# Two layer blocks on one core: the products that spread the HGRN norm's roots placed among a branch slot's products, and sixteen unread transposes ahead of the third norm's

## The reference, cut to what matters

```python
def hybrid_mixer(xn, ...):
    q, zf_fwd, zf_bwd, inp, og, hy, gates = split(xn @ w_in)
    o2 = hgrn2_chunk_scan(...)                  # forward and reversed
    o = o2[:B] + rev(o2[B:])
    o = rmsnorm(o, hgrn_norm_g).reshape(B, L, HGRN_WIDTH)    # over the 128 channels of each of 8 heads
    y_a = (o * silu(og)) @ w_branch_a
    y_b = (x0 * bidirectional_fftconv(v * x1, ...)) @ w_branch_b
    merged = sigmoid(g_a) * y_a + sigmoid(g_b) * y_b
    return merged @ w_out

h = h + hybrid_mixer(rmsnorm(h, norm_mix_g), ...)
h = h + peer_ffn(rmsnorm(h, norm_ffn_g), peer_w_q, subkeys, u, v)
```

## Time and profile before

| | us |
|---|---|
| median of 3 runs | 1563.37 |
| lowest, highest | 1561.97, 1563.64 |
| the profiled execution | 1565.21 |
| its span | 1563.4 |

### The profile page before, as it was taken

One profiled execution on the slowest core, in us unless ns is written; L12 is line 12 of the kernel. 1 busy time (PEld: TensorE's weight loads), 2 busy tenths in 40 slices (PEclk: granted clock), 3 DMA queues, 4 the chain that ended last, 5 costly groups with the idle time before them and its releaser, 6 DMA issues.

```text
span 1563.4 us, 28014 instructions
## 1 busy us (share of the span) xinstructions
PE 1531.3 (98%) x9966; PEld 1335.4 (85%) x9966; DVE 956.6 (61%) x1389; ACT 804.1 (51%) x1087; POOL 1190.6 (76%) x499
## 2 busy tenths in 40 slices
PE   7999999999999999999999999999999999999998
PEld 5688888887899989989899998888887778788886
DVE  5545366655432457744239960787878999954444
ACT  5456655557555565444554455555554444444443
POOL 6643598885897965558778998877777777788995
PEclk9999999999999999999999999999999999999999
DMA  8433465554554543335645555555554555566553
GB/s 279 163 122 103 150 222 187 189 186 164 187 187 158 167 135 99 119 121 185 212 157 179 185 180 184 175 168 171 171 175 162 175 166 175 169 227 191 196 191 121
DMA packets 72773, 267.85 MB, mean 171 GB/s; under 512 B 8177, under 2 KB 8449, under 8 KB 71745
## 3 DMA queue, kind: packets, MB, share of 16 engines
q1 hardware_dynamic: 70272, 253.99, 49.7%
q0 software_dynamic: 1568, 7.12, 1.3%
q10 hardware_dynamic: 864, 5.77, 0.9%
HBM read 263.70 MB, written 3.15 MB: 171 GB/s over the span
## 4 chain that ended last, share of the span: by engine, by line
PE 59%; POOL 17%; issue 15%; DVE 5%; DMA 2%; ACT 2%; POOLq 0%; DVEq 0%; ACTq 0%; SPq 0%
PE ps L1206 58%; POOL ring_lo L1266 17%; DMA ring<-in_stream 2%; DVE h_both L1949 1%; DVE onehots_i L1134 1%; ACT ring_hi L1696 1%; DVE big L959 1%; DMA big<-in_filt 0%; DVE onehot_j L1138 0%; DVE big L1153 0%; DVE big L1975 0%; DVE big L1977 0%; DVE big L1974 0%; ACT h_both L1709 0%; DVE h_both L1966 0%
## 5 line engine op out<-in xcount | busy, mean ns | idle before, releaser
L1266 POOL TENSOR_TENSOR ring_lo<-ring,ring_hi 128x1024 fp32r<-128x1024 f32 x472 | 1168.9, 2492 | 347.5 <-ACT ring_hi L1696 345.0
L1206 PE MATMUL ps<-h_both,ring_hi 128*128 128x256 f32 (+1 forms) x2944 | 744.9, 332 | 3.5 <-DVE h_both L1966 2.0
L1696 ACT CAST ring_hi<-ring 128x1024 fp32r<-128x1024 f32 x472 | 491.4, 1051 | 430.0 <-DMA ring<-in_stream 423.9
L1206 PE MATMUL ps<-h_both,ring_lo 128*128 128x256 f32 x2080 | 584.8, 281 | 0.0
L1206 PEld LDWEIGHTS ps<-h_both,ring_hi 128*128 128x128 f32 x2944 | 498.4, 190 | 59.3 <-issue 3.8
L1206 PE MATMUL ps<-ring_hi,h_both 128*128 128x512 f32 (+1 forms) x1408 | 428.4, 382 | 9.4 <-POOL ring_lo L1266 3.2
L1206 PEld LDWEIGHTS ps<-h_both,ring_lo 128*128 128x128 f32 x2080 | 395.9, 190 | 0.3
L1206 PEld LDWEIGHTS ps<-ring_hi,h_both 128*128 128x128 f32 x1408 | 259.9, 188 | 63.8 <-issue 8.6
L1206 PE MATMUL ps<-ring_lo,h_both 128*128 128x512 f32 (+1 forms) x704 | 265.8, 378 | 0.0
L1949 DVE TENSOR_TENSOR h_both<-big,h_both 128x512 fp32r<-128x512 f32 x64 | 130.5, 2041 | 102.6 <-ACT h_both L1709 102.2
L1206 PEld LDWEIGHTS ps<-ring_lo,h_both 128*128 128x128 f32 x704 | 132.7, 189 | 22.7
(11 more groups left out here) (303 smaller groups left out, 1376.8 us busy)
## 6 DMA issues: line engine op xcount, KB each, us to landing
ring<-in_stream SPq DMA_DIRECT2D x480, 512.0 KB, 3.7
residual<-big ACTq DMA_DIRECT2D x2, 1024.0 KB, 4.0
big<-residual ACTq DMA_DIRECT2D x2, 1024.0 KB, 5.8
x<-in_x SPq DMA_DIRECT2D x2, 512.0 KB, 5.3
big<-in_fdecay POOLq DMA_DIRECT2D x1, 1024.0 KB, 9.0
wrow<-in_post POOLq DMA_DIRECT2D x2, 512.0 KB, 5.3
big<-in_x ACTq DMA_DIRECT2D x1, 1024.0 KB, 5.0
big<-in_subkeys POOLq DMA_DIRECT2D x1, 1024.0 KB, 6.1
```

Source lines behind the costliest of these rows:

```text
L1206: return nc.tensor.matmul(out, lhsT, rhs, start=start, stop=stop, skip_group_check=True)
L1266: P.tensor_tensor(ring_lo[:, h % RING, :], ring[:, h % RING, :], ring_hi[:, h % RING, :].bitcast(fp32), ALU.subtract).then_inc(S["split_lo ...
L1696: A.copy(ring_hi[:, h % RING, :], ring[:, h % RING, :]).then_inc(S["split_hi"], 1)
```

## The change

The wait for the roots and the eight spreading products go from between slots 38 and 39 into slot 39: `spread(h)` is issued ahead of product k = h of the half j = 0, the wait with h = 0, `o_scale` after each second one as before. And sixteen 128 x 128 transposes of the identity into the first quarter of bank 3, which nobody reads before slot W_Q + 1 overwrites it, are issued between the output product and `norm_transposes(3)`.

```diff
--- before.py
+++ after.py
@@ -475,16 +475,21 @@
             last.then_inc(S["o_sums"], 1)
             channels(38, src=hyena_parts)
 
-            pe.wait_ge(S["o_rstd"], 1)
-            for h in range(8):
+            def spread(h):
+
+                if h == 0:
+                    pe.wait_ge(S["o_rstd"], 1)
                 last = mm(ps[:, 4 + h // 2, (h % 2) * 256:(h % 2 + 1) * 256],
                           ident[0:8, h:h + 1].broadcast_to([8, 128]), RS[0:8, :])
                 if h % 2:
                     last.then_inc(S["o_scale"], 1)
-            channels(39, src=hyena_parts)
+
+            channels(39, src=hyena_parts, ready=spread)
             for idx in range(40, 44):
                 channels(idx, src=hgrn_parts, ready=None if idx > 40 else lambda k: wait_operand("hgrn", k // 2 + 1))
             out_product(W_OUT2, merged_parts, lambda quarter: wait_operand("merged", quarter + 1))
+            for n in range(16):
+                nc.tensor.transpose(ps[:, 3, 0:128], ident[:, :], ident[:, :])
             norm_transposes(3)
             for s in range(8):
                 if s < 2:
```

## The result

The changed kernel takes 1572.11 us (median of 4 runs, 1571.61 to 1573.47) against 1562.76 for the kernel before in the runs beside it: a ratio of 1.0056, 95% interval 1.0039 to 1.0072, or 6.1 to 11.3 us more. It is slower, and beyond the range. The profiled execution took 1571.9 us for a span of 1570.1; that of before took 1565.21, so the two profiles are 6.7 us apart.

The account below looks back on a forecast made before the run. TensorE, busy 98% of the span, was taken to bound the kernel. Part 1's +1.56 us less part 2's 0.54 made +1.0 on the median of 1563.37: 1564.4 us, called no change, range 1561.2 to 1567.6.

Parts of the forecast that it names:

- the first one of the sum: Slot 39 with the spread among its products: if the clock holds, it ends at 699.2, 1.35 us earlier (bounds 0.8 and 3.3).
- Rival D: Slot 39's first half: eight-row products bring the clock down after three groups; +4.7 us, 1568.1; chance 0.15.
- its other term: Slot 39's eight groups, each three records and a spreading product: 1.05 us per group, bounds 0.80 and 1.12.
- The switch: Slot 39: extra cost of changing between record kinds around a lone spreading product, taken as 0.25 us, bounds nothing and 0.33.
- T: Start of VectorE's fourth scaling of the spread's results, forecast at 696.1 instead of 692.22.
- The chain behind the scalings: ScalarE, GpSimd, VectorE after T: GpSimd at T + 2.37 wins by 0.04 us, subtraction 4 ends at T + 8.1.
- A: The forecast: clock holds, GpSimd wins, slot 40 waits some 0.8 then 2.2 us; 1564.4 us; chance 0.40.
- C: As A, but slot 40's two waits bring the clock down; 1566.1 us, or 1567.8 with a fall twice as long; chance 0.15.
- B: VectorE gets in before GpSimd or alternation leaves no wait, slot 40 follows at once: -1.9 us, 1561.5; chance 0.30.
- Part 2: Sixteen transposes before the third norm: they cost nothing, keep the clock at 1.00, and win 0.54 us (0.11 and 0.43).
- part 1: Spread moved among slot 39's products: +1.6 us net, though about 3.1 us lost at half clock could be won.
- the cover over VectorE's subtractions: Slot 40: last subtraction ready at 701.55, wanted at 702.70, only 1.15 us of cover while slot 39 ran slow.

Follow-up runs that it names:

- e1: The changed kernel without the sixteen transposes, so the spread's move alone: ratio 1.0034 to the kernel before, median 1571.09 us against 1565.04.
- e3: The changed kernel with 128 active rows instead of 8 in the spreading products among slot 39's products: ratio 1.0014 to the kernel before, 1566.73 us.
- e5: The changed kernel run again, on another chip: ratio 1.0042 to the kernel before, 1572.0 us against 1565.39.
- e7: The kernel before with 32 active rows instead of 8 in its block of spreading products, no transposes: ratio 0.9998, 1566.77 us.
- e6: The changed kernel without transposes, one eight-row product ahead of every second product over both halves of slot 39: ratio 1.0058 to the kernel before, 1574.4 us.
- e4: The kernel before with 128 active rows in the spreading products, still one block ahead of slot 39, no transposes: ratio 1.0006, 1566.28 us.
- e8: The kernel before with a 128-row spread block, the sixteen transposes, and VectorE's four subtractions ahead of its branch products: ratio 1.0001, 1565.99 us.
- e2: The kernel before plus only the sixteen transposes, spread in one block as before: ratio 0.9988, 1564.13 us.
- e10: The changed kernel with 128-row spreading products among slot 39's and GpSimd held until VectorE's fourth subtraction: ratio 0.9975 to the kernel before, 1562.93 us.
- e11: The kernel before, unchanged, profiled a second time: 1565.04 us.
- e9: The kernel before with a 128-row spread block, the sixteen transposes, and GpSimd held until VectorE's fourth subtraction: ratio 0.9980, 1563.27 us against 1566.59.

## Why the prediction was wrong

1. **The failed step is the first one of the sum: "If the clock holds, slot 39 ends at ... 699.2: 1.35 us earlier".** It didn't hold: 0.50 for 13.65 us, and slot 40 5.63 us later against the spread's start. Rival D is what happened, at its place and from the fall it named (after three groups), and I gave it 0.15. Its reason was in the text (eight-row records alone did it before); the reason against, "full-height products stand between", rested on no row. e1 and e3 differ in the number of active rows and in the transposes alone, and e5 against e3 in the rows alone: 18.14 against 9.15 in stage (a). That is shown, with the limit said at e7. The step would also have failed with the clock held, by its other term: with groups of 1.17 as measured at full clock, its sum gives 12.15 for stage (a) (e6, whose clock held, has 12.2 without its wait), 0.36 earlier than before and not 1.35. By these figures I estimate that of the 5.63 us lost, about 3.0 are the longer time at half clock and 2.7 the eight switches: 18.14 is 9.15 (e3), 3.0 of switches and 6.0 of clock, and 12.51 is 9.20 (e4), 0.3 (the block's switch, as in e7) and 3.0.

2. **D was also under-sized:** +4.7 against +6.4 in the stages. Of the 1.7 between, 0.4 is stage (a), 5.63 for 5.2: a group is 1.17 for 1.05 at full clock and 2.08 for 1.9 at half. The switch was 0.37 and lay above its upper bound of 0.33. I had argued that a lone narrow product is spared some of the waits of a block of them; at 0.37 it was spared none. The other 1.3 is stage (b), where D had slot 40's operands in time: T came 13.25 us behind the spread's start and not 11.5, the last operand at 708.25, and slot 40 wanted it at 707.2.

3. **The chain behind the scalings was right**: GpSimd at T + 2.37, VectorE asking 0.04 later, the last subtraction done at T + 8.1, all as laid from the earlier trace rows. So was what A made of it: e3 and e6 show the waits that A forecast and, with them, the fall that C added. Had the clock held in slot 39, C would have been likelier than A or B. That is argued from two profiles, and in e4 and e8 a wait of 1.83 us brought no fall.

4. **Part 2 was right in the profile**: 0.11 and 0.43 won, transposes of 1.91 us under the wait with 0.38 left, clock at 1.00 from 751 to 757. It had said "nothing in a run in which the clock didn't fall", and still put the whole 0.54 into the sum: e1's norm kept its clock without the transposes, so the gain is that of some executions. The Trainium skill (TensorE: Matmul & The Clock Gate, "Part 4: PE-mode transpose") says that a transpose doesn't count as PE-busy in the same way. The rule, by which part 2 would be 0, isn't borne out: in the profiles with the sixteen transposes (changed, e2, e3, e5, e8 to e10) the norm ran at 1.00; of the six without, three fell (before, e4, e11) and three didn't (e1, e6, e7). Seven of seven against three of six points one way and is few.

5. **What part 1 could win was looked for in the wrong place.** The 3.1 us lost beside the spread are real (e4: 9.20 for 12.51, 3.3), but the cover over VectorE's subtractions was made of that loss: the earlier trace rows left 1.15 us of it. A faster TensorE alone gives 2.2 us back in stage (b), around a wait of 1.83 (e4, e8). Full rows and a held GpSimd together take the whole of it: a and b are 3.3 us shorter in e9. Full rows alone were worth nothing measurable (e4); GpSimd held alone was not tried.

What stays open: why the norm's fall comes in some executions and not in others, why waits of 1.8 us in slot 40 are followed by a fall in some and not in others, and why the spread's fall is 3.4 us long in one profile of the kernel before and 6.8 in another. e8 also has a fall of 3.4 us far from the change, at 1184.5. No run here separates these. The first comparison's difference of 9.35 us is above the stages' 6.4 and e5's 6.6; its interval contains both.

## What to carry to other kernels

Before moving an operation that is seen beside a clock fall, ask which of its properties does it, and test that property in place: here one changed operand, 128 active rows in place of 8 for the same columns, removed the fall and the switch, where moving the products had doubled the time at half clock (13.65 us for 6.83). Then ask what the lost time was covering: the gain appears only if the next-late engine, here VectorE, which takes turns with GpSimd, is freed as well. GpSimd had the slack to be told when to stay away: in e9 it began 3.9 us behind the fourth scaling (e8: 0.6), and TensorE still waited for nothing of it.

## What the runs showed that I had not expected

- Eight-row products brought the clock to 0.50 in a block (3.4 or 6.8 us), and also with one ahead of each full-height product (13.65 us in all three profiles); with one ahead of every second product slot 39 kept 1.00. Blocks of 32 and of 128 rows kept it too, for the same columns.
- A lone eight-row fp32 product among full-height ones cost 0.37 us beside its own passes at full clock, at every one; with 128 rows nothing.
- The stretches at 0.50 ahead of the final stores are 3.4, 6.8 or 13.65 us long in these profiles.
- Queued together, subtractions of 0.64 us on VectorE (two SBUF inputs) and of 2.4 us on GpSimd go in turn: 9.10 us for four in e8. The Trainium skill (SBUF — State Buffer, "SBUF: two separate sides") calls the pair of ports that the two share "an exclusive lock, not a bandwidth split"; e8 agrees and adds that neither gets ahead of the other.
